# A hybrid decoder step on one Trainium2 core: the few-token selector, paired partial sums, earlier joins and two-tile operations

## What is computed

```python
def swiglu(x, w_gate, w_up, w_down):
    return (jax.nn.silu(x @ w_gate) * (x @ w_up)) @ w_down

def chunk_gmlp(x, w_in, ln_g, ln_b, w_s, b_s, w_out):
    uv = jax.nn.gelu(x @ w_in)
    u, v = uv[..., :D_A], uv[..., D_A:]
    ...

def kv_project(h, pos, kv_norm, kv_w, k_norm_slc, k_norm_win):
    kv = (rmsnorm(h, kv_norm) @ kv_w).reshape(B, T, N_BRANCH, 2, N_KV_HEADS, HEAD_DIM)
    ...

# layer 0: h += chunk_gmlp(norm(h)); h += swiglu(norm(h))
# keys and values of three attention branches from h, once
# layer 1: h += attention(norm(h) @ b_w_in, keys, values) @ b_w_out; h += swiglu(norm(h))
```

## Time and profile before

| | us |
|---|---|
| median of 3 runs | 1587.46 (1587.44 to 1588.08) |
| the profiled execution | 1583.63 |
| its span, first to last instruction | 1581.8 |
| PE busy | 1528.0 (97%), 12766 matmuls |
| DVE busy | 1076.5 (68%) |
| ACT busy | 645.7 (41%) |
| POOL busy | 95.0 (6%) |
| mean granted clock of PE | 0.993 of full speed |

### The profile page before, as it was taken

How to read it: one execution, slowest core, us unless ns; L and a number is a source line. 1 busy time by engine, 2 the same in 40 slices (tenths; PEclk the granted TensorE clock), 3 DMA queues, 4 the chain that set the end, 5 groups by cost and what they waited for, 6 DMA issues and landing times.

```text
span 1581.8 us, 31230 instructions
## 1 busy us (share of the span) xinstructions
PE 1528.0 (97%) x12766; PEld 1439.3 (91%) x12766; DVE 1076.5 (68%) x1701; ACT 645.7 (41%) x1143; POOL 95.0 (6%) x155
## 2 busy tenths in 40 slices
PE   7999999999999999998999899998899999999998
PEld 6999999999999999997999756766699999999998
DVE  5338753368777878755256788977667968777952
ACT  6335221233333334334343667666453324333321
POOL 0000000000000000000000124544000000000000
PEclk9999999999999999999999999999999999999999
DMA  5247322322232323231224513104542222323232
GB/s 168 80 161 257 102 87 75 102 80 81 67 120 69 106 94 108 74 104 64 81 86 155 170 37 125 54 2 135 134 107 81 89 78 88 120 68 120 68 104 73
DMA packets 135821, 157.14 MB, mean 99 GB/s; under 512 B 11803, under 2 KB 119635, under 8 KB 135283
## 3 DMA queue, kind: packets, MB, share of 16 engines
q1 hardware_dynamic: 135618, 155.42, 31.1%
q10 hardware_dynamic: 80, 0.02, 0.0%
HBM read 149.58 MB, written 14.16 MB: 104 GB/s over the span
## 4 chain that ended last, share of the span: by engine, by line
PE 76%; DVE 14%; ACT 6%; issue 2%; POOL 0%; DMA 0%; DVEq 0%; SPq 0%; ACTq 0%
PE PS L718 39%; PE PS L748 11%; PE PS L949 11%; PE PS L1223 2%; PE PS L1140 2%; PE PS L1238 2%; DVE wlA L2257 1%; DVE wlB L2261 1%; ACT whA L1633 1%; PE PS L755 1%; PE PS L1195 1%; DVE wl L1954 1%; PE PS L1103 1%; DVE sums L2242 1%; DVE sums L2245 1%
## 5 line engine op out<-in xcount | busy, mean ns | idle before, releaser
L1460 ACT ACTIVATE wh<-raw 128x2048 fp32r<-128x2048 f32 (+2 forms) x90 | 143.4, 1593 | 194.2 <-PE PS L718 143.8
L1954 DVE TENSOR_TENSOR wl<-raw,wh 128x2048 fp32r<-128x2048 f32 (+2 forms) x90 | 170.2, 1891 | 70.9 <-ACT wh L1460 70.8
L2008 DVE TENSOR_TENSOR hT<-PS,hT 128x544 f32<-128x544 f32 (+1 forms) x104 | 75.2, 723 | 136.4 <-PE PS L718 135.8
L949 PE MATMUL PS<-opH,whA 128*128 128x272 f32 x512 | 148.7, 291 | 5.8 <-DVE sg L2270 3.0
L949 PE MATMUL PS<-opL,whA 128*128 128x272 f32 x512 | 148.1, 289 | 0.0
L949 PE MATMUL PS<-opH,wlA 128*128 128x272 f32 x512 | 147.8, 289 | 0.0
L748 PE MATMUL PS<-wh,act0h 128*128 128x256 f32 x448 | 129.6, 289 | 7.4 <-DVE sel_b L2091 7.4
L718 PE MATMUL PS<-act0h,wh 128*128 128x272 f32 x640 | 133.5, 290 | 0.4 <-DVE sg L2153 0.4
L718 PE MATMUL PS<-act0l,wh 128*128 128x272 f32 x640 | 132.3, 288 | 0.0
L718 PE MATMUL PS<-act0h,wl 128*128 128x272 f32 x640 | 132.3, 288 | 0.0
L748 PE MATMUL PS<-wl,act0h 128*128 128x256 f32 x448 | 127.0, 284 | 0.0
(11 more groups left out here) (403 smaller groups left out, 3926.9 us busy)
## 6 DMA issues: line engine op xcount, KB each, us to landing
raw<-in_ffn_w_gate SPq DMA_DIRECT2D x44, 512.0 KB
raw<-in_ffn_w_up SPq DMA_DIRECT2D x44, 512.0 KB
raw<-in_a_w_in SPq DMA_DIRECT2D x32, 512.0 KB
raw<-in_ffn_w_down SPq DMA_DIRECT2D x64, 256.0 KB
raw<-in_a_w_out SPq DMA_DIRECT2D x16, 512.0 KB
crows<-in_cache_kv_cmp SPq DMA_DIRECT2D x32, 256.0 KB, 2.9
cache<-in_state_kv_win SPq DMA_DIRECT2D x8, 1024.0 KB, 6.8
out_kv_win_sample<-in_state_kv_win SPq DMA_DIRECT2D x8, 1016.0 KB
```

Of the source, the lines that this page charges most:

```text
L949: mm = pe.matmul(PS[:, bank, 0:HALF], w, X[:, x, k, :], start=(k == 0 and not last and X is opH), stop=(k == 3 and last))
L1460: act.activation(wh[:, rs, 0:kn, :], raw[:, rs, 0:kn, :], ACT.Copy).then_inc(w_hi, 1)
L1954: dve.tensor_tensor(wl[:, rs, 0:kn, :], raw[:, rs, 0:kn, :], wh[:, rs, 0:kn, :].bitcast(F32), ALU.subtract).then_inc(w_ready, 1)
L2008: dve.tensor_tensor(h, psum_u(s, mt), h, ALU.add).then_inc(free[s], 1)
```

## The change

It has five edits. (1) `selector(sel_b, 3)` is called ahead of `last_segment` of layer 0 instead of behind it. (2) `item_b` in slot 0 makes its own partial sums and, after a wait for the raw weights of slot 1, those of the next block; slot 1 makes none, except as second item of a segment (`alone`). (3) On DVE `join_first` of the next item comes ahead of `sums(third)`. (4) For sevens ACT runs silu once on both tiles, behind `blocks_high`. (5) `multiply`, `products_high` and `products_low` handle both tiles in one operation each. Semaphore counts are kept.

```diff
--- before.py
+++ after.py
@@ -738,9 +738,9 @@
                     if mid is not None and k == KT // 2:
                         mid()
 
-        def item_b(rs, ps, n, use, X, kn=KT, fresh=None, mid=None, gated=False):
-
-            (xh, xl), few, part, f0, at_, sel = X
+        def item_b(rs, ps, n, use, X, kn=KT, fresh=None, mid=None, gated=False, alone=False):
+
+            (xh, xl), few, part, f0, at_, use0, sel = X
 
             def products(t, k):
                 a = k * T + t * P
@@ -749,10 +749,10 @@
                                    start=(k == 0 and W is wh and Xp is xh), stop=(k == KT - 1 and Xp is xl))
                 return mm
 
-            def partials():
+            def partials(r=rs):
                 for k in range(KT):
                     c = 32 * (k % 4)
-                    mm = pe.matmul(PS[c:c + 32, 4 * ps + 2, 0:CW], few[:, k, :], raw[:, rs, k, :],
+                    mm = pe.matmul(PS[c:c + 32, 4 * r + 2, 0:CW], few[:, k, :], raw[:, r, k, :],
                                    start=(k < 4), stop=(k >= 4))
                 mm.then_inc(f_mm, 1)
 
@@ -777,7 +777,12 @@
                 pe.wait_ge(f_sel, 3)
                 mm = gather()
             elif fresh is None:
-                partials()
+                if rs == 0:
+                    partials()
+                    pe.wait_ge(loaded[1], 64 * (use - use0 + at_ // 2 + 1))
+                    partials(1)
+                elif alone:
+                    partials()
                 pe.wait_ge(free[ps], 2 * use + 1)
                 for t in range(QT):
                     for k in range(KT):
@@ -809,7 +814,10 @@
                 item(0, 0, at[0], at[2], X, kn, fresh, mid)
                 if mid is not None:
                     pe.wait_ge(*mid.read)
-                item(1, 1, at[0] + 1, at[2], X, kn)
+                if item is item_b:
+                    item_b(1, 1, at[0] + 1, at[2], X, alone=True)
+                else:
+                    item(1, 1, at[0] + 1, at[2], X, kn)
                 done = 1
             with pe.Fori(0, turns - done) as i:
                 for s in range(2):
@@ -861,7 +869,7 @@
             tr.then_inc(x_tr, 1)
 
         pe.wait_ge(g_set, 2)
-        segment(item_b, at_v, 4, (act0, few_v, part_v, 0, at_v[0], sel_v), fresh=0)
+        segment(item_b, at_v, 4, (act0, few_v, part_v, 0, at_v[0], at_v[2], sel_v), fresh=0)
 
         def spread_and_turn():
 
@@ -998,11 +1006,11 @@
 
         ffn(0)
         pe.wait_ge(f_sel, 6)
-        segment(item_b, at_kv, 3, (act0, few_k, part_b, 8, at_kv[0], sel_b), fresh=2 * KT, mid=sum_squares(2, at_kv[2]))
+        segment(item_b, at_kv, 3, (act0, few_k, part_b, 8, at_kv[0], at_kv[2], sel_b), fresh=2 * KT, mid=sum_squares(2, at_kv[2]))
         pe.wait_ge(xn_ready, 4 * KT)
         pe.wait_ge(f_ready, 3)
         for q in range(NG):
-            item_b(q % 2, q % 2, at_q[0] + q, at_q[2] + q // 2, (act1, few_q, part_b, 14, at_q[0], sel_b), gated=(q == 3))
+            item_b(q % 2, q % 2, at_q[0] + q, at_q[2] + q // 2, (act1, few_q, part_b, 14, at_q[0], at_q[2], sel_b), gated=(q == 3))
             if q == 2:
                 pe.wait_ge(gw_lo, 1)
                 pe.wait_ge(free[1], 2 * at_q[2] + 4)
@@ -1615,6 +1623,10 @@
             act.wait_ge(free[0], 2 * it.use + mt + 3)
             act.activation(sg[:, mt, :], sg[:, mt, :], ACT.Silu).then_inc(g_act, 1)
 
+        def silu_both(it):
+            act.wait_ge(free[0], 2 * it.use + 4)
+            act.activation(sg[:, :, :], sg[:, :, :], ACT.Silu).then_inc(g_act, 2)
+
         def operands_high(l, k):
 
             act.wait_ge(x_made, 4 * l + k + 1)
@@ -1651,26 +1663,24 @@
 
         def products_high(it):
             X = ffn_pair(it.c)
-            for mt in range(2):
-                a = (2 * (it.j // 2) + mt) * T
-                act.wait_ge(v_up, it.m + mt)
-                act.activation(X[0][:, a:a + T], ug[:, mt, :], ACT.Copy).then_inc(v_uh, 1)
+            a = 2 * (it.j // 2) * T
+            act.wait_ge(v_up, it.m + 1)
+            act.activation(X[0][:, a:a + 2 * T], ug[:, :, :].rearrange("p m t -> p (m t)"), ACT.Copy).then_inc(v_uh, 1)
 
         def ffn(l):
             items = ffn_items(l)
             for e, it in enumerate(items[:-4]):
                 following, ahead = items[e + 1], items[e + 2]
                 gate = it.kind == "up" and it.j % 2 == 0
-                if gate:
+                if gate and it.m is None:
                     silu(it, 0)
-                if gate and it.m is None:
                     silu(it, 1)
                 if ahead.m is None:
                     split(ahead.rs, ahead.n, ahead.n // 2, it.unit, kn=ahead.kn)
                 else:
                     blocks_high(ahead, it)
                 if gate and it.m is not None:
-                    silu(it, 1)
+                    silu_both(it)
                 if following.m is not None:
                     first_out(following)
                 if it.m is not None and not gate:
@@ -2288,17 +2298,16 @@
             dve.tensor_tensor(flat, PS[:, 5:7, 0:HALF], flat, ALU.add).then_inc(free[it.rs], 2)
 
         def multiply(it):
-            for mt in range(2):
-                dve.wait_ge(g_act, it.up + 2 * (it.j // 2) + mt + 1)
-                dve.wait_ge(free[1], 2 * it.use + mt + 3)
-                dve.tensor_tensor(ug[:, mt, :], ug[:, mt, :], sg[:, mt, :], ALU.mult).then_inc(v_up, 1)
+            dve.wait_ge(g_act, it.up + 2 * (it.j // 2) + 2)
+            dve.wait_ge(free[1], 2 * it.use + 4)
+            dve.tensor_tensor(ug[:, :, :], ug[:, :, :], sg[:, :, :], ALU.mult).then_inc(v_up, 2)
 
         def products_low(it):
             X = ffn_pair(it.c)
-            for mt in range(2):
-                a = (2 * (it.j // 2) + mt) * T
-                dve.wait_ge(v_uh, it.m + mt)
-                dve.tensor_tensor(X[1][:, a:a + T], ug[:, mt, :], X[0][:, a:a + T].bitcast(F32), ALU.subtract).then_inc(up_done, 1)
+            a = 2 * (it.j // 2) * T
+            dve.wait_ge(v_uh, it.m // 2 + 1)
+            dve.tensor_tensor(X[1][:, a:a + 2 * T], ug[:, :, :].rearrange("p m t -> p (m t)"),
+                              X[0][:, a:a + 2 * T].bitcast(F32), ALU.subtract).then_inc(up_done, 2)
 
         def ffn(l):
             items = ffn_items(l)
@@ -2324,22 +2333,23 @@
                     products_low(it)
                 if ahead.m is not None:
                     sums_low(ahead)
+                if items[e + 1].m is not None:
+                    join_first(items[e + 1])
                 if third.m is not None:
                     sums(third)
                 if items[e + 1].m is not None:
-                    join_first(items[e + 1])
                     join_second(items[e + 1])
                 if e < 4:
                     operands_made(l, e)
             at = at_ffn[l]["down", LAST]
             if l == 0:
+                selector(sel_b, 3)
                 last_segment(at, 2)
             else:
                 segment(at, 2, residual, tail=False)
 
         spread_squares(1)
         ffn(0)
-        selector(sel_b, 3)
         g, X = NORM_OUT[2][1]
         for k in range(KT):
             low(X, g, k, NORM_AT[2] + KT + k)
```

## The result

| | before | after |
|---|---|---|
| median of 4 runs | 1587.77 us | 1566.93 us (1566.36 to 1570.29) |
| profiled execution | 1583.63 us | 1566.44 us |
| its span | 1581.8 us | 1564.7 us |

The ratio is 0.9881, 95% interval 0.9859 to 0.9902.

What follows compares the result with a forecast made beforehand. PE (matmul engine), busy 97% of the span, was taken as the bound, so edits pay only where it stalls. Gains 8.3 + 2.7 + 7.4 = 18.4 us gave 1565.2 profiled and 1569.1 median, range 1566.5 to 1572 (chance 0.63).

Steps and rivals of the forecast that it cites:

- Part 1: Key/value start: selector moved so PE need not wait behind DVE's queue; gain 8.3 us, bounds 6.9 and 8.7.
- Rival (c): Key/value start: PE stays held by DVE's queue, or the low clock remains; gain 5 there, 1572.5 us; chance 0.06.
- Part 2: Partial sums of two blocks together: one leaving of the narrow form saved, six pairs of 0.45, 2.7 us, bounds 0 and 3.5.
- so their starts cover 0.69: 0.046 apiece. That cost stays: Narrow partial sums (L755): the 16 records moved to the even block still cost 0.69 us per pair.
- the held query pair: First query pair: block 2 already waits 0.7 us for DVE's weight split, would wait 0.45 longer, so no gain.
- rival (b): Narrow partial sums: the pause belongs to the batch, so pairing gives 0; 1571.9 us; chance 0.12.
- Part 3: Seven-product items: join first and two-tile operations; 3.7 us per layer, 7.4 in both, bounds 1 and 8.4.
- the place I had named: Last up chunk, sixth item: weights ready at 646.5, PE asks at 646.0, so 0.5 us of the 3.4 are left.
- between -0.1 and +0.4: Up items, two-tile products: DVE waits 0.4 us before products_low, then saves 0.1; effect in that range, taken as 0.
- My sign of being wrong: Seven-product items: wrong if PE idles at L949 for sums_low, or if DVE idles before L2270 for PE.
- Rival (a): Sevens keep their pace, DVE and ScalarE awaiting each other's whole pair; only about 1 us there, 1575.5 us; chance 0.16.
- Rival (d): Sevens: join_first heads DVE's queue before PE's third product, delaying work behind it; at 0.75 us each 13 slower, 1600; chance 0.03.

Runs made afterwards that it cites:

- e1_selector: Kernel before with only the selector moved ahead of layer 0's last down segment; last down product to gather 13.93 us from 22.38, ratio 0.9939.
- e7_wait_at_gather: Kernel before, selector left in place on DVE, PE's wait for it moved from ahead of the segment to the gather; last down product to gather 14.55 us.
- e4_join: Kernel before with only the next item's first join moved ahead of the sums; feed-forward 243.62 and 243.63 us, 2.25 and 2.22 less per layer.
- e9_join_sooner: Changed kernel with join_first one place further ahead, in front of sums_low; feed-forward 242.72 and 242.74 us, 0.67 and 0.69 more per layer.
- e5_silu_behind: Kernel before with the join ahead of the sums and both silus, one per tile, behind the block copy; feed-forward 241.71 and 241.74 us.
- after_again: The changed kernel compared with the kernel before a second time; median 1568.4 us against 1585.05, ratio 0.989 (0.987 to 0.991).
- e3_sevens: Kernel before with only the seven-product edits (join first, silu behind block copy, two-tile operations); feed-forward 242.04 and 242.06 us, ratio 0.9941.
- e2_pairs: Kernel before with only the partial sums of two blocks taken together; gather to L1954 87.89 us instead of 88.55, ratio 0.9987.

## Why the prediction was right

I predicted 1569.1 us, a gain of 18.4, of which the profiled execution should show 1565.2. It took 1566.44, with a start 0.84 us later than before.

- **Part 1**, predicted 8.3 us, measured 8.45 (`e1_selector`). PE started at once, the clock stayed at 1.00 (worth 1.56 us for 1.4), and the new wait at the gather was 0.47 us, predicted 0.4. The split of the gain between queue and selector was shown by `e7_wait_at_gather`. Rival (c) fell.
- **Part 2**, predicted 2.7 us, measured 1.94. This is the term that was mis-sized. The step was "so their starts cover 0.69: 0.046 apiece. That cost stays": the second batch costs 0.86, four distances between groups of records and not three, and a pair gives 0.33 where I took 0.45. The mechanism held (11 pauses; the held query pair gave nothing and its wait rose from 0.7 to 1.0), and rival (b), no gain at all, fell. The 0.41 us of "idleness" was not all lost: PE's last group of narrow records starts inside it.
- **Part 3**, predicted 7.4 us, measured 7.6. The runs of four lost their 0.4 us each, and of the 3.4 us in the run of six 0.4 were left, predicted 0.5, at the place I had named, the split weights of the sixth item. The gate item gave 0.98 us for 1.0 in its chain. Inside the part I was wrong on one step: I took the two-tile products as 0 "between -0.1 and +0.4"; they cost 0.19 us per up item, and without them no wait is left. My sign of being wrong, PE idle at L949 for `sums_low`, did show (L957, `wlB`, two waits, the longest 0.2 us), at the one place and in the size that the sum had allowed for. Rival (a) fell, though `e4_join` shows how it would have looked: with the join alone PE's wait moves to the split weights and 2.2 us per layer are gained.
- **Rival (d)**, slower, fell, and `e9_join_sooner` puts a price on it: 0.7 us per layer one place further ahead.
- The pause ahead of L748 occurs once per leaving of L755's form, 11 times for 18, whatever the number of batches. The Trainium skill ("TensorEngine Tiling (Array Packing)", Key Properties), which I cited, says that a change of tiling mode drains the engine. The count fits that rule, but no run here shows that it is the cause. The gathers are listed as 128*32 too, and PE goes into and out of each of them with no pause, its starts 0.12 us apart (TensorE, before):

```profile
118.65 0.28 PE L748 MATMUL PS<-wh,act0l 128*128 128x256 f32 x1
118.77 0.28 PE L763 MATMUL PS<-part_vh,sel_v 128*32 128x256 f32 x1
118.89 0.28 PE L764 MATMUL PS<-part_vl,sel_v 128*32 128x256 f32 x1
119.00 0.28 PE L748 MATMUL PS<-wh,act0h 128*128 128x256 f32 x1
```

  So the narrow shape alone does not cost. L755 differs in that it writes four partition groups and takes unsplit operands in two records; which of these makes the 0.33 us, if either, is open.
- One VectorE operation of 1088 elements takes 1.29 us where two of 544 spanned 1.36, so a merged pair saves 0.07 us, and the wait of 0.40 that merging brought is larger. The Trainium skill ("VectorE: DVE Perf Modes", The TRN2 errata) would have made it 0.16; the measurement decides.
- The medians: I subtracted the gain from 1587.46. The first comparison came out 2.2 us lower than my number, only 0.4 us above the lower end of my range, the second 0.7 lower. Both differences are smaller than the spread of single executions (below). By the stages the gain was 18.0 us, 0.4 less than I forecast; that the median nevertheless came out below my number is chance.

## What to carry to other kernels

Look for what a waiting engine's releaser has in front of it in its own queue: three operations of 0.6 us together, at the end of DVE's queue, held PE for 7.4 us, and the cure was to issue them, or to place the wait, elsewhere. Where two engines hand work to each other, order each so that what the other can start on comes first; merging operations saves less than 0.1 us apiece here and can cost more by making the other engine wait for the whole. When you price a batch that is to be repeated, count from its start to the start of what follows, less the cost of the change: the distance from its first record to its last leaves one step out. And take an edit's worth from the stage of the trace that it touches when single executions spread more than the edit gives.

## What was not expected of the hardware

**The attention stage takes 288.1 to 292.9 us** in thirteen traces, whatever the edits (288.78 in before and after, 292.91 in `e1_selector`). Every other stage in the table repeats within 0.1 us where its code is the same, with two exceptions: the value blocks (below), and the stretch from the last down product to the gather where the gap was kept. There `e4_join` and `e5_silu_behind` took 0.5 and 0.3 us longer than the kernel before: 7.99 and 7.75 us for the first 48 products of the segment, for 7.45, at a granted clock of 0.71 and 0.74, for 0.78. So the attention stage may well be what spreads whole executions (1581.78 to 1589.63 for the kernel before in one series); without their traces that stays open. The table of stretches for the kernel before and then for `e1_selector` (us; busy PE, PEld, DVE, ACT, POOL; clock; DMA share; GB/s):

```profile
1060.00:1100.00 40.00, 36.86 (x419) 27.39 (x416) 30.61 (x74) 25.44 (x109) 22.56 (x48) 1.00 0.43 131
1100.00:1160.00 60.00, 52.33 (x714) 42.72 (x712) 42.58 (x105) 36.25 (x102) 0.00 (x0) 0.97 0.44 113
```

```profile
1060.00:1100.00 40.00, 34.94 (x368) 26.27 (x370) 29.14 (x74) 24.07 (x101) 17.89 (x40) 0.96 0.41 133
1100.00:1160.00 60.00, 54.38 (x722) 45.09 (x715) 41.62 (x96) 34.60 (x91) 0.00 (x0) 0.94 0.50 124
```

In `e1_selector` the granted clock is 0.96 and 0.94 where it was 1.00 and 0.97, so more of this stage ran at the lower level, 1.2 GHz. The other long one, `after_again` (291.91 us), has 0.91 and 0.94 in the same two stretches. What decides that was not tried.

**A clock granted early was no gain.** In `e3_sevens` PE had the full clock already from 16 to 24 us, reached the first value gather sooner, waited there 2.37 us instead of 0.88 for DVE, and was then at 0.89 where the kernel before had 1.00. Again the same view, the kernel before and `e3_sevens`:

```profile
16.00:24.00 8.00, 8.00 (x58) 7.96 (x59) 6.49 (x16) 5.50 (x11) 0.62 (x1) 0.79 0.01 2
33.00:45.00 12.00, 12.00 (x106) 11.74 (x106) 4.25 (x7) 4.58 (x8) 0.00 (x0) 1.00 0.28 90
```

```profile
16.00:24.00 8.00, 8.00 (x71) 7.96 (x70) 6.37 (x16) 5.50 (x11) 0.62 (x1) 1.00 0.01 2
33.00:45.00 12.00, 12.00 (x96) 11.22 (x89) 4.25 (x7) 4.46 (x8) 0.00 (x0) 0.89 0.28 90
```

The gather came at the same time in both (31.77 and 31.65 us), and the value blocks behind it took 1.57 us longer. `e2_pairs` has the same wait of 2.37 us, and its value blocks took 1.50 us longer than those of the changed kernel, which has the same code there.
